# Merge products of a decoder trunk as three passes over parts

## The reference, cut to what matters

```python
h = rms_norm(x, mix_g)
p = h @ w_in                       # slabs of the four branches, and 4 x 1024 gate columns
y_b = mixer_b(p)                   # (512, 256) for each branch b
m = sum(sigmoid(p_gate_b) * (y_b @ w_out_b) for b in branches)
x = x + m @ w_o
x = x + relu(rms_norm(x, mlp_g) @ w_up) ** 2 @ w_down
```

## Time and profile before

| what | us |
|---|---|
| median of 3 runs | 2148.43 (2147.41 to 5273.4) |
| profiled execution, its own time | 2149.84 |
| its span, first to last instruction | 2148.1 |
| PE busy | 2071.7 |
| DVE busy | 1080.4 |
| ACT busy | 752.4 |
| POOL busy | 738.0 |
| mean granted PE clock | 0.984 |

### The profile page before, as it was taken

One profiled execution on the slowest core, in us unless ns is written; L12 is line 12 of the kernel. 1 busy time (PEld: TensorE's weight loads), 2 busy tenths in 40 slices (PEclk: granted clock), 3 DMA queues, 4 the chain that ended last, 5 costly groups with the idle time before them and its releaser, 6 DMA issues.

```text
span 2148.1 us, 34922 instructions
## 1 busy us (share of the span) xinstructions
PE 2071.7 (96%) x14648; PEld 1603.9 (75%) x14648; DVE 1080.4 (50%) x1788; ACT 752.4 (35%) x1152; POOL 738.0 (34%) x550
## 2 busy tenths in 40 slices
PE   5999999999999999999989999999999999999997
PEld 3778787766767888888867877877576778888886
DVE  5775553797833422222356845458957333222223
ACT  3541512334353342323243334133453433332322
POOL 1540212331223444444435213133222244444442
PEclk7999999999999999999989999999999999999998
DMA  4320111221312333323232111022113123332331
GB/s 168 98 87 16 60 32 53 87 87 46 101 47 83 106 99 98 93 93 98 91 106 83 57 36 55 23 74 92 49 46 128 55 81 97 98 98 89 98 96 61
DMA packets 52266, 170.04 MB, mean 79 GB/s; under 512 B 5648, under 2 KB 13968, under 8 KB 51600
## 3 DMA queue, kind: packets, MB, share of 16 engines
q1 hardware_dynamic: 50928, 162.75, 23.9%
q0 software_dynamic: 1184, 5.07, 0.6%
HBM read 160.45 MB, written 7.34 MB: 78 GB/s over the span
## 4 chain that ended last, share of the span: by engine, by line
PE 86%; DVE 9%; ACT 3%; issue 1%; DMA 1%; SPq 0%; DVEq 0%; ACTq 0%
PE bank_a L468 14%; PE bank_a L469 13%; PE bank_a L472 13%; PE bank_v L472 7%; PE bank_v L468 7%; PE bank_v L469 7%; PE bank_v L608 5%; PE bank_v L530 4%; PE bank_v L736 2%; PE bank_f L541 1%; DVE arena L1422 1%; PE bank_v L718 1%; PE bank_f L547 1%; PE bank_a L727 1%; PE bank_a L867 1%
## 5 line engine op out<-in xcount | busy, mean ns | idle before, releaser
L429 POOL TENSOR_TENSOR w_lo<-ring,w_hi 128x512 fp32r<-128x512 f32 x536 | 731.6, 1386 | 1289.5 <-ACT w_hi L1102 1289.5
L468 PE MATMUL bank_a<-h_hi,w_hi 128*128 128x512 f32 x1376 | 561.8, 408 | 7.8 <-DVE h_lo L1455 4.8
L469 PE MATMUL bank_a<-h_lo,w_hi 128*128 128x512 f32 x1376 | 541.0, 393 | 0.0
L1102 ACT ACTIVATE w_hi<-ring 128x1024 fp32r<-128x1024 f32 x268 | 281.5, 1050 | 234.5 <-DVE arena L1959 220.1
L472 PE MATMUL bank_a<-h_hi,w_lo 128*128 128x512 f32 x1376 | 340.0, 389 | 0.0
L468 PEld LDWEIGHTS bank_a<-h_hi,w_hi 128*128 128x128 f32 x1376 | 260.6, 189 | 89.4 <-issue 24.0
L469 PEld LDWEIGHTS bank_a<-h_lo,w_hi 128*128 128x128 f32 x1376 | 261.4, 190 | 60.2 <-issue 8.3
L472 PEld LDWEIGHTS bank_a<-h_hi,w_lo 128*128 128x128 f32 x1376 | 258.6, 188 | 53.9
L468 PE MATMUL bank_v<-parts,w_hi 128*128 128x512 f32 x640 | 254.4, 398 | 1.4 <-DVE parts L1930 1.4
L469 PE MATMUL bank_v<-parts,w_hi 128*128 128x512 f32 x640 | 253.4, 396 | 0.0
L1422 DVE TENSOR_TENSOR sg<-bank_v,sg 128x512 f32<-128x512 f32 x112 | 77.5, 692 | 326.5 <-PE bank_v L472 256.5
(11 more groups left out here) (273 smaller groups left out, 2369.9 us busy)
## 6 DMA issues: line engine op xcount, KB each, us to landing
ring<-in_w SPq DMA_DIRECT2D x268, 512.0 KB, 3.5
out_ring<-in_w SPq DMA_DIRECT2D x64, 128.0 KB, 3.5
x_dram<-arena SPq DMA_DIRECT2D x2, 2048.0 KB, 7.6
arena<-x_dram SPq DMA_DIRECT2D x2, 2048.0 KB, 9.8
arena<-in_x SPq DMA_DIRECT2D x2, 1024.0 KB, 8.5
arena<-tabs POOLq DMA_DIRECT2D x4, 512.0 KB, 4.8
out_x<-arena SPq DMA_DIRECT2D x2, 1024.0 KB, 4.2
par<-in_par POOLq DMA_DIRECT2D x2, 937.0 KB, 7.1
```

What stands on the lines that cost most here:

```text
L429: ins = nc.gpsimd.tensor_tensor(w_lo[:, g % SPLIT, ks, :], raw, w_hi[:, g % SPLIT, ks, :].bitcast(F32), ALU.subtract)
L468: mm(b[:], w_hi[:, s, k, :], hi[:, k, :], start=k == 0, stop=False)
L469: mm(b[:], w_hi[:, s, k, :], lo[:, k, :], start=False, stop=False)
L1102: act_fn(w_hi[:, g % SPLIT, :, :], ring[:, g % RING, :, :], ACT.Copy).then_inc(S["split_hi"], 1)
```

## The change

The merge product is no longer done in float32 but in parts. `yo` is replaced by `y_hi` and `y_lo`: DVE rounds (copy) and subtracts. For rwkv and gdn it does so in two halves of 128x512 right after the branch's output (`parts_of`); for the attentions ACT takes the transposed output into `yt`, and DVE parts 128x256 for each query tile, tiles 0 to 2 two steps after ACT's take, and tile 3 right after the attention, ahead of the selection (`parts_of_rows`). For the outgoing weights ACT makes `out_hi` in `split_next`, right after `w_hi` of a merge unit; it waits there for the load. POOL makes `out_lo` after `w_lo` of that unit, in the place of the raw weights. PE waits for `out_lo` and `y_lo` and runs six passes a tile. The raw weights, `out_hi` and `out_lo` have five buffers where there were six, so the load of tile n waits until tile n - 5 is merged.

```diff
-OUT_RING = 6
+OUT_RING = 5
...
-        out_ring = sb("out_ring", [P, OUT_RING, 2, P])
+        out_hi = sb("out_hi", [P, OUT_RING, 2, P], F32R)
+        with nc.sbuf_tensor("out_ring", [P, OUT_RING, 2, P], F32) as out_ring:
+            pass
+        out_lo = sb("out_lo", [P, OUT_RING, 2, P], F32R)
...
-        yo = sb("yo", [P, 2, 2, T])
+        y_hi = sb("y_hi", [P, 2, T], F32R)
+        y_lo = sb("y_lo", [P, 2, T], F32R)
...
@@ POOL, after w_lo of unit g
+                if UNITS[u][0] == "merge":
+                    n = merges_to(g)
+                    pool.wait_ge(S["ow_hi"], n + 1)
+                    slot = n % OUT_RING
+                    nc.gpsimd.tensor_tensor(out_lo[:, slot, :, :], out_ring[:, slot, :, :], out_hi[:, slot, :, :].bitcast(F32), ALU.subtract).then_inc(S["ow_lo"], 1)
@@ PE, merge_outputs
-                    pe.wait_ge(out_here[n % OUT_RING], 16 * (n // OUT_RING + 1))
+                    pe.wait_ge(S["ow_lo"], n + 1)
+                    hi, lo = out_hi[:, n % OUT_RING], out_lo[:, n % OUT_RING]
                     for k in range(2):
-                        ins = mm(b[:], out_ring[:, n % OUT_RING, k, :], yo[:, slot, k, :], start=k == 0, stop=k == 1)
+                        mm(b[:], hi[:, k, :], y_hi[:, k, :], start=k == 0, stop=False)
+                        mm(b[:], hi[:, k, :], y_lo[:, k, :], start=False, stop=False)
+                    for k in range(2):
+                        ins = mm(b[:], lo[:, k, :], y_hi[:, k, :], start=False, stop=k == 1)
@@ PE, ahead of the merges of each branch (rwkv shown)
-                pe.wait_ge(S["r_out"], at(l, "r_out", 1))
+                pe.wait_ge(S["r_yl"], at(l, "r_yl", 2))
@@ ACT, split_next, after w_hi
+                    if UNITS[g % NU][0] == "merge":
+                        n = merges_to(g)
+                        if n >= OUT_RING:
+                            act.wait_ge(S["mg_done"], n - OUT_RING + 1)
+                        act.wait_ge(out_here[n % OUT_RING], 16 * (n // OUT_RING + 1))
+                        act_fn(out_hi[:, n % OUT_RING, :, :], out_ring[:, n % OUT_RING, :, :], ACT.Copy).then_inc(S["ow_hi"], 1)
@@ ACT, take_output
-                act_fn(yo[:, slot, :, qt * P:(qt + 1) * P], b[:, 0:2 * P].rearrange("p (f n) -> p f n", n=P), ACT.Copy).then_inc(S[x + "_y"], 1)
+                act_fn(V["yt"][:, :, qt * P:(qt + 1) * P], b[:, 0:2 * P].rearrange("p (f n) -> p f n", n=P), ACT.Copy).then_inc(S[x + "_y"], 1)
@@ DVE
+            def parts_of(l, x, src):
+                for f in range(2):
+                    v.tensor_copy(y_hi[:, f, :], src[:, f, :]).then_inc(S[x + "_yh"], 1)
+                    dve.wait_ge(S[x + "_yh"], reached(x + "_yh"))
+                    v.tensor_tensor(y_lo[:, f, :], src[:, f, :], y_hi[:, f, :].bitcast(F32), SUB).then_inc(S[x + "_yl"], 1)
+
+            def parts_of_rows(l, x, src, qt):
+                rows = slice(qt * P, (qt + 1) * P)
+                dve.wait_ge(S[x + "_y"], at(l, x + "_y", qt + 1))
+                v.tensor_copy(y_hi[:, :, rows], src[:, :, rows]).then_inc(S[x + "_yh"], 1)
+                dve.wait_ge(S[x + "_yh"], reached(x + "_yh"))
+                v.tensor_tensor(y_lo[:, :, rows], src[:, :, rows], y_hi[:, :, rows].bitcast(F32), SUB).then_inc(S[x + "_yl"], 1)
...
@@ DVE, attention, end of step i
+                    if i - 2 in OUTPUT_STEPS:
+                        parts_of_rows(l, x, V["yt"], OUTPUT_STEPS.index(i - 2))
...
@@ DVE, rwkv output (gdn alike)
-                v.tensor_tensor(yo[:, 0, :, :], R["o"], R["g"], MUL).then_inc(S["r_out"], 1)
+                v.tensor_tensor(R["o"], R["o"], R["g"], MUL).then_inc(S["r_out"], 1)
                 dve.wait_ge(S["r_out"], reached("r_out"))
+                parts_of(l, "r", R["o"])
...
                 attention(l, "m", Mv, 96 ** -0.5, lambda qt: Mv["bias"][:, (3 - qt) * P:T])
+                parts_of_rows(l, "m", Mv["yt"], 3)
                 go_on(9)
...
                 attention(l, "d", Dv, C ** -0.5, lambda qt: Dv["bias"][:, qt, 0:(qt + 1) * P] if qt else cst("causal"))
+                parts_of_rows(l, "d", Dv["yt"], 3)
```

More of the change, by code:

```diff
@@ L277, in build @@
             ("m_ss", 16), ("m_p", 16), ("m_pt", 16), ("m_o", 16), ("m_y", 4),
+            ("r_yh", 2), ("g_yh", 2), ("r_yl", 2), ("g_yl", 2), ("m_yh", 4), ("d_yh", 4), ("m_yl", 4), ("d_yl", 4), ("ow_hi", 32), ("ow_lo", 32),
             ("mg_sig", 32), ("mg_raw", 4), ("mg_done", 32), ("mg_hi", 8), ("mg_lo", 8), ("wo_done", 8), ("up_relu", 32), ("up_sq", 32), ("up_hi", 32), ("up_done", 32), ("g_zs", 1), ("r_s0", 1), ("g_s0", 1), ("down_done", 8 * QUARTERS),
@@ L360, in build @@
             iq=ar(15, (4, T)), q=ar(19, (2, T)), k=ar(21, (2, T)), vf=ar(23, (2, T)), v=ar(25, (TT, 256)), tab=ar(27, (2, T)), ik=ar(29, (T,)),
-            tmp=ar(35, (T,)), ss=ar(11, (4, T)), pt=ar(15, (3, TT, P)), y=ar(24, (2, 256)),
+            tmp=ar(35, (T,)), ss=ar(11, (4, T)), pt=ar(15, (3, TT, P)), y=ar(24, (2, 256)), yt=ar(27, (2, T)),
         )
@@ L365, in build @@
             tab=ar(27, (2, T)), tmp=ar(29, (T,)), bias=ar(32, (T,)), kr=ar(33, (T,)),
-            ss=ar(15, (4, T)), pt=ar(34, (3, TT, P)), y=ar(23, (2, 256)),
+            ss=ar(15, (4, T)), pt=ar(34, (3, TT, P)), y=ar(23, (2, 256)), yt=ar(27, (2, T)),
         )
@@ L903, in indexed_merge @@
                         index_pair()
+                    pe.wait_ge(S["g_yl"], at(l, "g_yl", 2))
                     merge_outputs(1, numbers)
@@ L959, in _ @@
                 more.append(gate(l, 1, 3))
-                pe.wait_ge(S["m_y"], at(l, "m_y", 4))
+                pe.wait_ge(S["m_yl"], at(l, "m_yl", 4))
                 merge_outputs(0, numbers)
@@ L973, in _ @@
                 more.append(gate(l, 3, 3))
-                pe.wait_ge(S["d_y"], at(l, "d_y", 4))
+                pe.wait_ge(S["d_yl"], at(l, "d_yl", 4))
                 merge_outputs(1, numbers)
@@ L1118, in norm_root, with attention @@
                         act_fn(h_hi[:, k, :], mg[:, k, :], ACT.Copy).then_inc(S["n_hi"], 1)
-            def attention(l, x, V, slot, fill):
+            def attention(l, x, V, fill):
                 steps = [(qt, h) for qt in range(TT) for h in range(H)]
@@ L1137, in attention, with take_output @@
                     if i in OUTPUT_STEPS:
-                        take_output(x, slot, OUTPUT_STEPS.index(i))
+                        take_output(x, V, OUTPUT_STEPS.index(i))
                     fill(i)
-            def take_output(x, slot, qt):
+            def take_output(x, V, qt):
                 act.wait_ge(a_full, filled.next())
                 b = filled.bank()
-                act_fn(yo[:, slot, :, qt * P:(qt + 1) * P], b[:, 0:2 * P].rearrange("p (f n) -> p f n", n=P), ACT.Copy).then_inc(S[x + "_y"], 1)
+                act_fn(V["yt"][:, :, qt * P:(qt + 1) * P], b[:, 0:2 * P].rearrange("p (f n) -> p f n", n=P), ACT.Copy).then_inc(S[x + "_y"], 1)
             def inverse_roots(dst, scales, eps, sums, roots):
@@ L1349, in _ @@
                 merge_sig(l)
-                attention(l, "m", Mv, 0, lambda i: piecewise_sig(l, i))
+                attention(l, "m", Mv, lambda i: piecewise_sig(l, i))
                 late_sig(l, 2)
                 merge_sig(l, 1)
-                take_output("m", 0, 3)
+                take_output("m", Mv, 3)
                 merge_sig(l, 1)
@@ L1356, in _ @@
                 merge_sig(l)
-                attention(l, "d", Dv, 1, lambda i: piecewise_sig(l, i))
+                attention(l, "d", Dv, lambda i: piecewise_sig(l, i))
                 late_sig(l, 4)
                 merge_sig(l, 1)
-                take_output("d", 1, 3)
+                take_output("d", Dv, 3)
                 merge_sig(l, 1)
@@ L1782, in _ @@
                 stt(G["o"], G["o"], pr("gdn_g", 0), G["sq2"], MUL, MUL)
-                v.tensor_tensor(yo[:, 1, :, :], G["o"], G["z"], MUL).then_inc(S["g_out"], 1)
+                v.tensor_tensor(G["o"], G["o"], G["z"], MUL).then_inc(S["g_out"], 1)
                 dve.wait_ge(S["g_out"], reached("g_out"))
+                parts_of(l, "g", G["o"])
                 dve.wait_ge(tab_d_here, 16 * (l + 1))
```

## The result

The changed kernel takes 2163.43 us (median of 4 runs, 2162.96 to 2164.43), the kernel before 2147.92 beside it. The ratio is 1.0076, 95% interval [1.0063, 1.0088]. One of the four runs of the kernel before took 5273.4 us and does not count in the ratio. The forecast was 5 us longer by its sum, and 15.5 came: inside the stated range of 2141 to 2167 and with the sign right, but the forecast size is a third of the measured one, and 2163.4 lies outside the 2147 to 2160 that the favoured case was given. The profiled execution has a span of 2161.9 us, 13.8 more than before.

A forecast was written before the change was run, and what follows sets the result against it. PE was taken to bound most of the kernel, DVE the selection's gdn and mla merges. The stretches summed to -2.5 us a layer, 5.0 us longer for two: 2153.4 from the median, stated as 2154, range 2141 to 2167.

The forecast's parts named there:

- the favoured case: The prediction's own sum of stretches, 5.0 us longer, stated as 2154 us, own range 2147 to 2160, chance 58%.
- A: Layer up to 414 us (rwkv merges): PE saves 2.85, less ACT's added rounding; gain of 2.0 us a layer.
- B: From 414 to 515 us (gdn merges): DVE leads and POOL's new subtractions collide with it; loss of 1.6 us a layer.
- C: The first attention: DVE's parting fits in idle time, ACT's extra roundings cost most of a 0.3 us loss a layer.
- D: From 549 to 597 us (mla merges): DVE waits for y to part tile 3; loss of 4.8 us a layer.
- E: The second attention: parting fits in DVE's idle time, ACT's roundings cost most of a 0.3 us loss a layer.
- F: The dsa merges, on PE's path: saving of 2.85 less 0.35 for the output product's wait; gain of 2.5 us a layer.
- the distance named as the test: From the first attention's end to the second's start: 4 to 6 us longer if right, unchanged or shorter if wrong.
- 0.6 is paid: After the rwkv scan: two ACT roundings of 0.3 us each stand ahead of what PE already waits 1.66 us for.
- 7 x 0.65 x 0.6: From 414 to 515 us: seven POOL subtractions of 0.65 us cost DVE about 62% of their length, 2.5 us.
- Rival 3: POOL's low part blocks DVE fully in the gdn and mla merges: 12 us more, 2166 us; chance 16%.
- fits: Within the attentions: DVE's copy of 0.35 and subtraction of 0.42 fit its 1.37 us idle before the next score.

The follow-up runs named there:

- round later: The changed kernel with ACT rounding the outgoing weights of the two rwkv tiles behind both norm roots, not in front: 2157.38 us, ratio to the kernel before 1.0045.
- filling it: The changed kernel with 8 unused products on TensorE ahead of its 2.12 us wait for ACT after the rwkv scan: 2156.61 us, ratio to the kernel before 1.0045.
- the wait is filled: Changed kernel with mla tile 3 parted after five selection steps, two rwkv roundings behind the norm roots, and 14 overwritten products in the second attention's scores: 2142.61 us.
- the one with the parting later: The changed kernel with DVE parting query tile 3 of the mla attention after five selection steps instead of ahead of them: 2149.73 us, ratio to the kernel before 1.0010.
- ACT's copy: The kernel before with one more 128x256 copy on ACT for each merge unit, on spare data: 2152.42 us, ratio 1.0022.
- four passes: The changed kernel without the two passes of out_lo with y_hi, four instead of six a tile: 2150.80 us, ratio to the kernel before 1.0013.
- both moves: The changed kernel with mla tile 3 parted after five selection steps and two rwkv roundings held behind the norm roots: 2145.38 us, ratio to the kernel before 0.9986.

## Why the forecast had the sign and not the size

Per layer, gain positive, forecast against the stretches:

| step | forecast | measured |
|---|---|---|
| A | +2.0 | about 0 (A2 +2.25, A1 -2.25) |
| B | -1.6 | +0.4 |
| C | -0.3 | -0.4 |
| D | -4.8 | -6.9 |
| E | -0.3 | -2.2 |
| F | +2.5 | +1.9 |
| sum | -2.5 | -7.2 |

**What was right.** D turns the sum, and through the wait named: y came at 556.56, where 556.6 was said. By the distance named as the test the second attention starts 6.9 us later, where 4 to 6 was said. A new pass is 0.233 where 0.227 was said, and A2 gave 2.6 to 2.9 in every kernel with all six passes but the changed one itself (161.4 to 161.5, against 164.0 to 164.3 without the change). The sixth tile was rounded at 577.4, where 578.5 was said; PE did wait for outgoing parts, named as a sign of being wrong, but for 2.3 us in the whole execution and where DVE leads. C was right to 0.1. The shorter PE is worth nothing in D.

**What was luck.** The terms missed by more than the total. A, D, E and F came out worse by 2.0, 2.1, 1.9 and 0.6 a layer, and B better by 2.0; without B's error the sum would be 4 us further off. The range held because it was drawn wide for other cases.

**A, the step "0.6 is paid".** 0.6 it was. What the sum lacked is the clock: 1.65 us more, seen in both layers of the changed kernel, removed by shortening the wait (round later) and by filling it. The changed kernel's own profile loses another 0.6 in A2, in small products between 318 and 326; none of the five other kernels with the same code there has that, and no view names its cause. That stays open.

**D, too small by 2.1.** The delay was put at 8.6 and came to 9.4 when the selection resumed: the two operations that part took 2.23 us in a collision, where 1.4 was allowed. Two more operations behind it met the low part of 558.50 and the next w_lo pair of 561.66 (0.89 for 0.42, 1.33 for 0.36 undisturbed), some 1.4 more. The relief at the end was near the 3.8 said: the idle 1.93 of the earlier trace rows went, and so did the collision at 590.74 (0.43 now).

**B, the step "7 x 0.65 x 0.6".** As a price of the collisions alone it was nearly right: GpSimd's operation by itself met five operations with two SBUF operands, not seven, but for longer (0.99 against 0.65), and B's longer operations sum to 2.15 where 2.5 was said. What the step lacked is that a delayed DVE meets the next w_lo pairs at another moment: four operations became shorter by 1.35, and idle time took 0.35. That leaves about 0.4, and of the 0.93 that PE's saving was to give, 0.5 is left after it, where B gained 0.36. That collisions would move was in the sum for D, and was left out here. Whether they move in one's favour can't be read off a single length; here they did. Rival 3, full blocking, had the total nearly right (2166) and the place wrong: GpSimd's part alone costs B 0.39, where it priced 5.2, and nothing that can be measured in the whole.

**E, the step that "fits".** The parting did nearly fit: 0.5 is left when the wait is filled. The other 1.7 of the 2.2 are the clock behind PE's wait. The kernel before with DVE work alone shows such a loss without the change, and the filled wait takes it away. In other words, in D the mla tiles' PE saving was not worth nothing, as I wrote, but less than nothing: it lengthened an idle time that costs clock.

**F.** F gained 1.9 of PE's 2.85, where 2.5 was said. PE waited 1.3 us for the parts of the output product, 0.7 in the earlier trace rows: that is 0.6 against the 0.35 allowed. The rest was not tested.

## What to carry to other kernels

A saving on the leading engine is worth its length only where that engine leads; where it doesn't, the saved time becomes a wait, and behind TensorE's waits of 2.1 to 7.4 us here the clock mostly fell, and that cost another 1.4 to 2.4 us. When a change puts a new reader of a late value into an in-order queue, put it behind work that doesn't need the value: here five selection steps moved ahead of it were worth 13.7 us. Of a collision between GpSimd and VectorE, ask first which VectorE operation stands there, and then what its delay does to the collisions behind it: here 2.15 us of losses came with 1.35 of gains. Count both over the whole stretch before calling either the cost.

## What the runs showed of the hardware

- The wait of 2.12 us on PE was followed by a granted clock of 0.50 (1.2 GHz) in six of eight cases: both layers of the changed kernel and of the one with the parting later, one layer of two with ACT's copy and with four passes. The wait of 1.66 at the same place was followed by none in six (before, roundings later, both moves). So 0.5 us more of waiting cost 0.6 us or 2.2 us, and which of the two is not the same in each layer.
- In a stretch at 0.50, gate passes start 0.43 us apart, at 1.00 they start 0.23 apart. The Trainium skill (TensorE: Matmul & The Clock Gate, Part 1) gives 426.7 and 215.7 ns for 512 columns; the trace agrees with the first; in place of the second, the passes here stand 227 to 233 ns apart.
- A copy of 128x512 from SBUF to SBUF took 0.89 us on DVE on average and the subtraction 1.04, where 0.7 undisturbed was assumed; in A and before B they lay in idle time.
